# Five wide matmuls a k step in place of six in 188 of 208 dense tiles of a two-layer decoder step

## The reference, cut to what matters

```python
for layer in range(2):
    h = rmsnorm(x, norm_mix_g[layer])
    if layer == 0:   # proj = h @ w_in_ab -> pooling mixer | differential attention over pages
        y = concat(pool_mix(...), diff_attn(...)) @ w_out_ab
    else:            # proj = h @ w_in_cd -> short gated conv | dilated attention, three groups
        y = concat(b_gate * short_conv(c_gate * hc), dilated(...)) @ w_out_cd
    x = x + y
    x = x + square(relu(rmsnorm(x, norm_mlp_g[layer]) @ w_up[layer])) @ w_down[layer]
y_prompt, y_sample = rmsnorm(x, norm_out_g)
```

## Time and profile before

| | |
|---|---|
| Device time, median of 3 runs | 1790.25 us (1789.88 to 1797.45) |
| Profiled execution: span from first to last instruction | 1793.1 us |
| Profiled execution: own device time | not listed apart; the three runs above are all there are |
| Busy: PE, PEld, DVE, ACT, POOL | 1736.8, 1623.3, 954.7, 548.6, 159.4 us |
| Matmuls (as many weight loads) | 15035 |
| Granted TensorE clock over the span | 0.996 |

### The profile page before, as it was taken

How to read it: one execution, slowest core, us unless ns; L and a number is a source line. 1 busy time by engine, 2 the same in 40 slices (tenths; PEclk the granted TensorE clock), 3 DMA queues, 4 the chain that set the end, 5 groups by cost and what they waited for, 6 DMA issues and landing times.

```text
span 1793.1 us, 36785 instructions
## 1 busy us (share of the span) xinstructions
PE 1736.8 (97%) x15035; PEld 1623.3 (91%) x15035; DVE 954.7 (53%) x1454; ACT 548.6 (31%) x1075; POOL 159.4 (9%) x212
## 2 busy tenths in 40 slices
PE   7998999999999999999999999999999999999998
PEld 6995667899999999999898898878799999999998
DVE  4336776655353433444587774677665435343454
ACT  4114556432121222231511413443133212122222
POOL 0710000320000000020000000012012000000002
PEclk9999999999999999999999999999999999999999
DMA  8219999337676767544368678523033767422221
GB/s 277 71 50 363 351 353 346 124 118 257 234 257 234 257 233 257 187 131 158 96 198 284 211 253 274 197 83 102 33 121 120 278 227 260 173 79 88 75 91 55
DMA packets 167162, 338.82 MB, mean 189 GB/s; under 512 B 9178, under 2 KB 116500, under 8 KB 165437
## 3 DMA queue, kind: packets, MB, share of 16 engines
q1 hardware_dynamic: 164691, 249.74, 41.3%
q0 software_dynamic: 2240, 87.41, 13.0%
q10 hardware_dynamic: 114, 0.03, 0.0%
HBM read 324.36 MB, written 100.19 MB: 237 GB/s over the span
## 4 chain that ended last, share of the span: by engine, by line
PE 86%; DVE 7%; ACT 2%; DMA 2%; issue 1%; SPq 1%; ACTq 0%; DVEq 0%
PE pp L667 55%; PE pp L977 16%; PE pp L727 2%; PE pp L926 1%; DMA kvring<-in_cache_b_kv 1%; PE pp L741 1%; PE pp L761 1%; PE pp L1084 1%; PE pp L1131 1%; PE pp L1180 1%; PE pp L1109 1%; DVE stat L1668 1%; DVE pp L1666 1%; ACT e_p L2163 1%; DMA vring<-in_cache_d_kv 1%
## 5 line engine op out<-in xcount | busy, mean ns | idle before, releaser
L1943 ACT ACTIVATE whi<-raw 128x1024 fp32r<-128x1024 f32 x208 | 220.6, 1060 | 899.7 <-PE pp L667 687.7
L667 PE MATMUL pp<-a_hi,whi 128*128 128x288 f32 x1280 | 275.8, 297 | 1.0 <-DVE zbuf L1335 0.7
L667 PE MATMUL pp<-a_lo,whi 128*128 128x288 f32 x1280 | 274.6, 296 | 0.0
L667 PE MATMUL pp<-a_hi,wlo 128*128 128x288 f32 x1280 | 274.4, 296 | 0.0
L1292 DVE TENSOR_TENSOR wlo<-raw,whi 128x1024 fp32r<-128x1024 f32 x208 | 256.0, 1231 | 30.5 <-ACT whi L1943 30.4
L667 PE MATMUL pp<-b_hi,whi 128*128 128x288 f32 x1152 | 247.0, 296 | 0.0
L667 PE MATMUL pp<-b_lo,whi 128*128 128x288 f32 x1152 | 247.0, 296 | 0.0
L667 PE MATMUL pp<-b_hi,wlo 128*128 128x288 f32 x1152 | 246.9, 296 | 0.0
L1351 DVE TENSOR_TENSOR x<-x,pp 128x576 f32 (+1 forms) x80 | 60.4, 755 | 295.1 <-PE pp L667 284.0
L667 PEld LDWEIGHTS pp<-a_hi,whi 128*128 128x128 f32 x1280 | 206.6, 189 | 2.3 <-issue 1.7
L667 PEld LDWEIGHTS pp<-a_lo,whi 128*128 128x128 f32 x1280 | 206.7, 189 | 0.0
(11 more groups left out here) (304 smaller groups left out, 2062.9 us busy)
## 6 DMA issues: line engine op xcount, KB each, us to landing
kvring<-in_cache_b_kv SPq DMA_DIRECT2D x128, 512.0 KB, 5.6
out_new_d_sample<-in_cache_d_kv POOLq DMA_DIRECT2D x32, 2040.0 KB, 8.5
raw<-in_w_up SPq DMA_DIRECT2D x32, 1024.0 KB, 5.4
raw<-in_w_down SPq DMA_DIRECT2D x32, 1024.0 KB, 5.2
kring<-in_cache_d_kv SPq DMA_DIRECT2D x104, 256.0 KB, 3.3
vring<-in_cache_d_kv SPq DMA_DIRECT2D x104, 256.0 KB, 5.3
raw<-in_w_in_cd SPq DMA_DIRECT2D x24, 1024.0 KB, 5.2
out_new_d_sample<-in_cache_d_kv POOLq DMA_DIRECT2D x8, 2016.0 KB, 8.3
```

The costliest lines, as they stand in the source:

```text
L667: last = pe.matmul(acc_h[s][:, h, :], w[s][:, k, :], m[:, k, NH * h:NH * h + NH], start=(at_ == 0 and n == 0), stop=(at_ == KT_N - 1 and n ...
L1943: act.activation(whi_v[j], raw_v[q // 2][:, :, j, :], ACT.Copy).then_inc(whi_ready, 1)
```

## The change

The cut through the 576 columns moves from 288 + 288 to 320 + 256 (`CUT`), and the accumulator moves with it: it is now 576 columns in one piece, 320 at the end of the pair's first bank (`left`) and 256 at the start of its second (`right`). The second bank's other 256 columns (`low`) are new work space. `whi*hi` and `whi*lo` of the right part are now one matmul of 512 columns over the whole second bank: its moving operand is read in two pieces of 256, from the high and from the low half of one buffer (`a_both`), and its result stands in `right` and `low`. A k step is then 320 + 320 + 512 + 320 + 256 columns, five matmuls, 1728 columns as before. At the end of the tile `low` must be added to `right`: DVE's new `fold` copies `low` to on-chip memory and adds it to `right` in PSUM, ahead of the evacuation; `down_folded` adds `low` straight to the right part of `x`. The evacuations become one piece of 576 columns, `evac_streams` two in place of three.

20 tiles keep six matmuls (`six`), cut at 320 + 256: the 8 of OA and the last 12 of CD. The other 188 take five: AB 16, both MLPs 128, CD 36, OC 8.

```diff
+        CUT = 320
+        acc_t = [pp[i][:, 512 - CUT:512 - CUT + N] for i in range(2)]
+        acc_lr = [(pp[i][:, 512 - CUT:512], pp[i][:, 512:512 + N - CUT]) for i in range(2)]
+        acc_pair = [pp[i][:, 512:1024] for i in range(2)]
+        acc_low = [pp[i][:, 512 + N - CUT:1024] for i in range(2)]
...
+            def five(s, k, parts, first, last):
+
+                lhs_hi, lhs_lo = whi_v[s][:, k, :], wlo_v[s][:, k, :]
+                left, right = acc_lr[s]
+                pe.matmul(left, lhs_hi, parts[:, 0, k, 0:CUT], start=first, stop=False)
+                pe.matmul(left, lhs_hi, parts[:, 1, k, 0:CUT], start=False, stop=False)
+                pe.matmul(acc_pair[s].rearrange("p (c n) -> p c n", c=2), lhs_hi, parts[:, :, k, CUT:N], start=first,
+                          stop=False)
+                pe.matmul(left, lhs_lo, parts[:, 0, k, 0:CUT], start=False, stop=last)
+                return pe.matmul(right, lhs_lo, parts[:, 0, k, CUT:N], start=False, stop=last)
...
@@ dense() of PE @@
-                            for n, (w, m) in enumerate(((whi_v, m_hi), (whi_v, m_lo), (wlo_v, m_hi))):
-                                for h in range(2):
-                                    last = pe.matmul(acc_h[s][:, h, :], w[s][:, k, :], m[:, k, NH * h:NH * h + NH],
-                                                     start=(at_ == 0 and n == 0),
-                                                     stop=(at_ == KT_N - 1 and n == 2))
+                            last = five(s, k, parts, at_ == 0, at_ == KT_N - 1)
...
@@ tile() of PE, CD @@
+                    if T >= T_CD + 36:
+                        last = six(s, k, ahk, alk, k == 0, k == KT_N - 1)
+                    else:
+                        last = five(s, k, a_parts, k == 0, k == KT_N - 1)
...
@@ DVE @@
+            def fold(G, q, skipped, spare):
+
+                out, low_ = acc_lr[q % 2][1], spare[:, (N - CUT) * (q % 2):(N - CUT) * (q % 2) + N - CUT]
+                dve.tensor_copy(low_, acc_low[q % 2]).then_inc(folded, 1)
+                dve.wait_ge(folded, folds(G, q, skipped) + 1)
+                dve.tensor_tensor(out, out, low_, ALU.add).then_inc(folded, 1)
+                dve.wait_ge(folded, folds(G, q, skipped) + 2)
...
-                dve.tensor_tensor(z.rearrange("p (h c) -> p h c", h=2), acc_h[j], r_h, ALU.mult).then_inc(acc_free, 1)
+                fold(G, q, skip, low_part)
+                dve.tensor_tensor(z, acc_t[j], rnorm[:, :], ALU.mult).then_inc(acc_free, 1)
...
+            def down_folded(skip, G, i, q):
+
+                xr = x[:, ds(i * (4 * N) + (q * N + CUT), N - CUT)]
+                dve.tensor_tensor(xr, xr, acc_low[q % 2], ALU.add).then_inc(folded, 2)
+                dve.wait_ge(folded, folds(G, q, skip) + 2)
+                down(G, i, q)
...
-                project(0, q, dp[:, :, 0:L0], rl(a0), rl(rnorm[:, 0:NH]))
-                project(0, q, dp[:, :, L0:32], rl(a1[:, 0:SEQ - NH]), rl(rnorm[:, NH:SEQ]))
-                project(0, q, dst[:, SEQ:N], a1[:, SEQ - NH:NH], rnorm[:, SEQ:N]).then_inc(acc_free, 1)
+                fold(T_CD // 4, q, 8, orun1)
+                project(0, q, dp, rl(acc_[:, 0:SEQ]), rl(rnorm[:, 0:SEQ]))
+                project(0, q, dst[:, SEQ:N], acc_[:, SEQ:N], rnorm[:, SEQ:N]).then_inc(acc_free, 1)
...
-                        project(gi, q, halves_of(dst_tile(gi, q)), acc_h[q % 2], r_h).then_inc(acc_free, 1)
+                        fold(T_CD // 4, 12 * gi + q, 8, e_p1[3])
+                        project(gi, q, dst_tile(gi, q), acc_t[q % 2], rnorm[:, :]).then_inc(acc_free, 1)
```

More of the change, by code:

```diff
@@ L17 @@
 from contextlib import ExitStack, contextmanager
+from functools import partial
 import numpy as np
@@ L650, in _, with six, dense @@
         def _(pe):
-            def dense(group, n_groups, m_hi, m_lo, ready, ready_base, hook=None, peel=False, order=range(KT_N),
+            def five(s, k, parts, first, last):
[7 more added lines that the diff above has]
+                return pe.matmul(right, lhs_lo, parts[:, 0, k, CUT:N], start=False, stop=last)
+            def six(s, k, m_hi, m_lo, first, last_):
+                for n, (w, m) in enumerate(((whi_v, m_hi), (whi_v, m_lo), (wlo_v, m_hi))):
+                    for out, cols in zip(acc_lr[s], (slice(0, CUT), slice(CUT, N))):
+                        last = pe.matmul(out, w[s][:, k, :], m[:, k, cols], start=(first and n == 0),
+                                         stop=(last_ and n == 2))
+                return last
+            def dense(group, n_groups, parts, ready, ready_base, hook=None, peel=False, order=range(KT_N),
                       before=None):
@@ L823, in _ @@
             transpose_x(3)
-            dense(lambda i: i, 1, ahk, alk, a_ready, 0, peel=True, before=opening)
+            dense(lambda i: i, 1, a_parts, a_ready, 0, peel=True, before=opening)
             pe.wait_ge(s_hist, 32)
@@ L923, in out_tile @@
                         ready(k)
-                    for n, (w, m) in enumerate(((whi_v, ohk), (whi_v, olk), (wlo_v, ohk))):
-                        for h in range(2):
-                            last = pe.matmul(acc_h[T % 2][:, h, :], w[T % 2][:, k, :], m[:, k, NH * h:NH * h + NH],
-                                             start=(k == 0 and n == 0), stop=(k == KT_N - 1 and n == 2))
+                    last = six(T % 2, k, ohk, olk, k == 0, k == KT_N - 1)
                 if ks[-1] == KT_N - 1:
@@ L962, in _ @@
             out_tile(T_OA + 3, range(8))
-            dense(lambda i: i + (T_OA // 4 + 1), 1, ohk, olk, b_ready, 0)
+            for T in range(T_OA + 4, T_OA + 8):
+                out_tile(T, range(8))
             mlp(0, T_M0)
@@ L974, in tile @@
                         pe.wait_ge(a_ready, 16 + (k + 1))
-                    for n, (w, m) in enumerate(((whi_v, ahk), (whi_v, alk), (wlo_v, ahk))):
-                        for h in range(2):
-                            last = pe.matmul(acc_h[s][:, h, :], w[s][:, k, :], m[:, k, NH * h:NH * h + NH],
-                                             start=(k == 0 and n == 0), stop=(k == KT_N - 1 and n == 2))
+                    if T >= T_CD + 36:
+                        last = six(s, k, ahk, alk, k == 0, k == KT_N - 1)
+                    else:
+                        last = five(s, k, a_parts, k == 0, k == KT_N - 1)
                     if k == KT_N - 1:
@@ L1244, in _ @@
                     prompt_attention(gi)
-            dense(lambda i: i + T_OC // 4, 2, bhk, blk, b_ready, 40, peel=True, order=(0, 1, 4, 5, 6, 7, 2, 3))
+            dense(lambda i: i + T_OC // 4, 2, b_parts, b_ready, 40, peel=True, order=(0, 1, 4, 5, 6, 7, 2, 3))
             mlp(1, T_M1)
@@ L1610, in evac_streams @@
             def evac_streams(q):
-                L0 = NH // 16
                 dst = dst_tile(0, q)
@@ L1917, in _ @@
             dve.wait_ge(x_spilled, 32)
-            dense(lambda i: i + T_OC // 4, 2, down, fin_post(3, G_MLP + 8), static=True)
+            dense(lambda i: i + T_OC // 4, 2, partial(down_folded, 20), fin_post(3, G_MLP + 8), static=True)
             mlp(1, T_M1)
```

73 lines of the change are left out of this document (38 added, 35 removed).

## The result

The changed kernel takes 1798.33 us in the median of 16 runs (1796.03 to 1802.44), the kernel before 1793.23 us in 16 runs (1789.88 to 1797.45). The ratio is 1.003, with a 95% interval of 1.0022 to 1.0038: slower by 0.3%, where 0.5% faster was forecast. 1504 matmuls went, as foretold (15035 to 13531), and the time grew all the same. It lies 16.7 us above the forecast of 1781.6 and just above the 1798 at which the widest range ended; 3.0 of the 16.7 are the base, since the three runs of before that the forecast started from had their median at 1790.25 and sixteen have it at 1793.23. The size of the change is told here by ratios, which don't depend on that base.

What follows compares the result with a forecast made beforehand. PE's dense matmuls were taken to bound the kernel: 19.0 us gained less 10.4 us of exposed folds gave 8.6 us less, 1784.5 against the profiled span and 1781.6 us as median. Its own range was 1777 to 1786, the widest 1775 to 1798.

Steps and rivals of the forecast that it cites:

- A per-matmul 13.4: Dense matmul streams: each matmul costs 13.4 ns beside one cycle a column, at 288 and at 512 columns alike.
- 1416 k steps, x 13.4 ns = 19.0 us: Gain on PE: one matmul less in each of the 1504 k steps, without 40 hidden and 48 paced by DVE.
- The rule of the Trainium skill: Warm matmul gap of N / 2.4 + 2.5 ns; gain of 3.5 us in place of 19.0, time 1797.
- excess by columns or two pieces: Rival: excess grows with columns, or the two-piece operand costs the removed matmul's price; 1797 to 1801 us; chance 0.09.
- The load rival: Rival: the narrow 256-column matmul is bound by its weight load at 133.4 ns; 1807 us; chance 0.09.
- The fold's own size: DVE's copy and addition of 256 columns at a tile's end, with waits: about 0.93 us.
- Its exposed places: Where PE already waits for an evacuation, as at starts of AB, MLPs and CD: about 0.93 us more each.
- the half fold: Last tile of all, before the addition to `x` on which the final norm waits: 0.5 us lost.
- From tile 5 on ... covered: Page tiles from 5 on: DVE idles 1.57 us in one tile, 0.32 + 0.76 in the next, covering the fold.
- Page tiles: Page tiles of CD: the fold outlasts DVE's idle time before the first page of tiles 2 to 4; 1.7 us lost.
- the prompt's attention: In CD, three times, score blocks and DVE's later work wait for the last tile's evacuation; 2.7 us lost.
- DVE binds the page tiles: Rival: all 16 page tiles pay up to 0.93 us each; 1795 us at worst, 1788 at half; chance 0.14.

Runs made afterwards that it cites:

- five_345: Changed kernel with five matmuls of 352, 352, 344, 340 and 340 columns a k step in tiles of loops and groups; 1787.5 us in a single run.
- no_folds: Changed kernel with the fold of the overhanging 256 columns left out everywhere; 1782.47 us, ratio 0.9945 to the kernel before.
- one_piece: Changed kernel with the 512-column matmul reading one run of 512 columns in place of two of 256; 1799.36 us in a single run.
- page_six: Changed kernel with six matmuls and no fold in the 16 page tiles; 1791.74 us, ratio 0.9997 to the kernel before.
- six_with_folds: Changed kernel with six matmuls a k step in all tiles, the folds' VectorE instructions kept in place; 1808.36 us, ratio 1.0086 to the kernel before.
- output_first: Changed kernel with the next tile's sample output updated ahead of `wlo` in tiles beside sample attention; 1794.47 us, ratio 1.0008 to the kernel before.

## Why the prediction was wrong

**A matmul's price: the term that was mis-sized on the gain.** "A per-matmul 13.4" was right as the price of a matmul among equals: five_345 has 787 ns. The step that failed is pricing the 512-column matmul of a mixed k step at the same 13.4, from one start-to-start row that was good to 5 ns. It shows 231 ns in the stream of 320s, which was inside the 225 to 235 allowed for, the 320 behind the narrow one shows 149 for 147, and the k step got 793.3 in place of 787. The term "1416 k steps, x 13.4 ns = 19.0 us" became 1504 x 6.7 ns = 10.0 us; no_folds has it (1416 k steps would give 9.4, which its interval doesn't tell apart). The rule of the Trainium skill that the prediction weighed ("TensorE: Matmul & The Clock Gate", "Back-to-back issue gap") makes a removed matmul worth 2.5 ns; the section itself gives that formula for a single isolated matmul, and in the streams here it doesn't hold. A removed matmul was worth 6.7 ns in the changed kernel's split and 13.3 in five_345's, so the rule is too low in both; that the kernel nonetheless came out near its 1797 is luck, the page tiles' doing and the low base's.

**The rival "excess by columns or two pieces"** was half right: a part of the excess went with the width, but neither in proportion (six of 256 and five of 320 pay the same 13.3) nor by the pieces (one_piece). **The load rival** is refuted at 256 columns (120 ns); a floor of 113.3 ns stands at 192 and 224.

**The fold's own size** was right: 0.91 us for 0.93. **Its exposed places** were right too where PE had waited before: each grew by 0.82 to 0.96. In DVE's row of the last tile the half fold stands for 0.46, as foretold:

```profile
1784.38 0.42 DVE L1392 TENSOR_TENSOR x<-x,pp 128x256 f32<-128x256 f32 x1 [4.58 <-PE pp L669]
1784.84 0.75 DVE L1387 TENSOR_TENSOR x<-x,pp 128x576 f32<-128x576 f32 x1
```

**"From tile 5 on ... covered"** is the other step that failed. The matmul's price alone would have left the kernel at +0.4 us, this step alone at -3.6; both together make +5.4. Page tiles were priced at 1.7 us. page_six shows 7.5, of which 0.9 is the fold of tile 111, priced elsewhere (with the prompt's attention), so 6.6 against 1.7, and the 15.4 of six_with_folds against 10.4 agrees; output_first brings 3.9 of it back by itself. The prediction looked only for idle time of DVE before the first page. It didn't ask what lies between the fold and that idle time, and whether somebody waits for it: the update of the sample output was waited for, with nothing to spare. Six times PE then idled 0.76 to 0.77, and the idle time of DVE that followed was as long as before. So the folds cost 15.4 us in place of 10.4. The rival "DVE binds the page tiles" named the right stretch and, at half, nearly the right size (1788, 6.5 us above the forecast, where 5 were measured), but the mechanism is one late instruction in every second tile from the sixth on, not a full DVE: moving that instruction ahead of `wlo` gave back 3.9 us with every fold in place.

The sum as it was measured: -10.0 + 15.4 = +5.4, against -19.0 + 10.4 = -8.6. Nine of the 14 us between them are the matmul's price and five the page tiles. Against the forecast of 1781.6 us the base of three runs adds the other 3.

## What to carry to other kernels

When a change puts work on an engine that is off the critical path, list what stands behind the new work in that engine's queue up to the next idle time, and for each of these look at when its result is taken: a consumer that starts as soon behind it as one that had to wait (0.15 us here) has no slack, even if it shows no wait. Price an instruction's fixed cost from a stream with the new mix of sizes, not from one isolated pair of starts, when the gain is the small difference of two large numbers. And where an added step is exposed at a few places, keep the old form there: 20 of 188 tiles and an earlier fold at four places turned 0.3% slower into 0.4% faster.
